# Gated recurrence: the last multiplication of keys and queries moved from VectorE to ScalarE, block by block

## The chip, the cores and the metric

The kernel runs on one core of a Trainium2 chip. Its engines work side by side, each through its own list of instructions, and they wait for each other through semaphores: PE (TensorE, matrix products), DVE (VectorE), ACT (ScalarE), POOL (GpSimd) and SP (SyncE, which here only starts transfers). The metric is the device time of one execution in microseconds (us); the time of a kernel is the median of its runs.

## What is computed

One step of a two-layer decoder, for 1024 prompt tokens and 8 x 8 sample tokens. Layer 0 runs stick-breaking attention and, beside it, a gated recurrence (HGRN2) of 4 heads with 128 key and 128 value channels; layer 1 is retention. The change touches the recurrence alone:

```python
def gla_chunk_scan(q, k, v, log_f, s0, chunk):
    def step(S, inp):
        qc, kc, vc, gc = inp
        bcum = jnp.cumsum(gc, axis=2)
        o_inter = jnp.einsum('bhtk,bhkv->bhtv', qc * jnp.exp(bcum), S)
        diff = bcum[:, :, :, None, :] - bcum[:, :, None, :, :]
        decay = jnp.exp(jnp.where(mask, diff, -jnp.inf))
        scores = jnp.einsum('bhtk,bhsk,bhtsk->bhts', qc, kc, decay)
        o_intra = jnp.einsum('bhts,bhsv->bhtv', scores, vc)
        blast = bcum[:, :, -1, :]
        S_new = jnp.exp(blast)[..., None] * S + jnp.einsum('bhsk,bhsv->bhkv', kc * jnp.exp(blast[:, :, None, :] - bcum), vc)
        return S_new, o_inter + o_intra
```

A key is multiplied by all gates that follow it in its chunk, a query by all gates up to it. The gates `f` stand per channel and token.

## The kernel before

The program is a row of stages, each closed by a barrier of all engines: input projection of layer 0, attention, the recurrence (`hgrn_now`, some 134 us from 839.7 to 973.9 us of the profiled execution), then the output projection of layer 0 together with the input projection of layer 1, and last retention with its output projection.

In `hgrn_now` the channels lie on the 128 partitions and the tokens along the rows: `k[h]`, `q[h]`, `f[h]` are 128 x 1088 (1024 prompt tokens, 64 sample tokens). A chunk has 128 tokens, so there are NCH = 8. The decay between two tokens is never formed. Instead the scores are computed in NLEV = 8 levels. Level 0 takes each token with itself. Between levels, `move(h, j)` on DVE (L1747 to L1753) multiplies, in every block of 2 x 2^j tokens, the keys of the first half by the product of the gates of the second half, and the queries of the second half by the product of the gates of the first half. The products of 2^j gates stand in `e[h]`, where POOL has built them (`first.products`). Level i then gives the scores between the two halves of blocks of 2^i tokens: on PE into `near` (levels 0 to 5) or `far` (6 and 7), and DVE (`pick`) or ACT copies them out. After level 7 comes `move(h, 6)`, the last, by the products of 64 gates: from then on a key carries all gates up to the end of its chunk, and a query all from the start. These are what the state of the recurrence needs. Head 0 has its tensors in the tile `first_place`; the others in `hg_k`, `hg_qd`, `hg_e`. The queries as moved are `qd`.

What follows a head's levels is its `rest(h)`: PE turns the keys (L1878, L1882, into `ku`), ACT copies them to `kd_tm` (L1711, L1716) and puts far and picked scores in place (L1713, L1720, L1723), PE makes the updates of the state (L1889) and of the samples' states (L1895), DVE chains them (`states`, L1787 and L1790, L1795), PE makes the outputs (L1905, L1907 and, for the samples, L1920 and L1922), and a norm over each head goes ACT (squares, L1693), PE (sums, L1865), ACT (L1702, L1704), DVE (`finish`, L1777, L1779).

The order is written out by hand, and is the same list on every engine: heads start 4 levels apart, so level i of head h stands beside level i + 4 of head h - 1. `run` goes through it and puts one piece of `rest` behind each level: `rest(0)` runs with heads 1 and 2, `rest(1)` begins when head 3 begins, `rest(2)` when head 3 is alone (two pieces to a level), and `rest(3)` follows at the end. Before a new `rest` begins, the one before is finished. An engine works strictly down its list, so what stands behind a waiting instruction waits too. In `rest(h)` PE waits for the last move of the keys before it turns them (L1870), and for that of the queries before the outputs (L1899).

Of the kernel before, what the change touches and what calls it, by code (L numbers as in the profile page):

```python
# [23 lines left out]
ACT = mybir.ActivationFunctionType  # L24
# [3 lines left out]
P = 128  # L28
# [797 lines left out]
class FirstHead:  # L826
# [7 lines left out]
    NM = 7  # L834
# [681 lines left out]
def hgrn_now(nc, first, q_fm, sig_fm, neg_fm, v_tm, gate_fm, out_gain, state_in, state_prompt, state_samples, mix_fm, consts):  # L1516
# [8 lines left out]
    with nc.cleanup_on_exit(), ExitStack() as ctx:  # L1525
# [3 lines left out]
        sem = lambda n: nc.alloc_semaphore(f"hg_{n}")  # L1529
        ps = lambda n, s: ctx.enter_context(nc.psum_tensor(f"hg_{n}", s, F32))  # L1530
        NM, NCH, NG = first.NM, TP // P, 2
# [25 lines left out]
        v_in, gate_in, s0_in = ([sem(f"{n}{h}") for h in range(HB)] for n in ("v_in", "g_in", "s_in"))  # L1557
        f_done, k_done, qd_done, e_done = first.f_done, first.k_done, first.qd_done, first.e_done
        scored, picked, k_moved, q_moved = sem("scored"), sem("picked"), sem("k_moved"), sem("q_moved")
        far_read, placed = sem("far_read"), sem("placed")  # L1560
        turned, held, updates, updates_s, state_done = sem("turned"), sem("held"), sem("updates"), sem("updates_s"), sem("state")
        vx_done, dec_done, s1_done, s_left = sem("vx"), sem("dec"), sem("s1"), sem("s_left")
# [7 lines left out]
        order = [(h, s - APART * h) for s in range(APART * (HB - 1) + NLEV) for h in range(HB) if 0 <= s - APART * h < NLEV]  # L1570
        nth = {x: i for i, x in enumerate(order)}
        nth_pick = {x: i for i, x in enumerate(x for x in order if x[1] < NPICK)}
        nth_move = {(h, i - 1): n for n, (h, i) in enumerate(x for x in order if x[1] >= 1)}

        def run(level, rest):

# [92 lines left out]
        @block.scalar  # L1669
        def _(act):  # L1670
            act.wait_ge(eps_set, 1)

            def level(h, i):
                if i == 0 and h + 1 < HB:
                    act.wait_ge(sig_in[h + 1], 16)
                    act.wait_ge(neg_in[h + 1], 16)
                    first.gates(nc, h + 1, f[h + 1][:], k[h + 1][:])
                if i == NLEV - 1:
                    s = scores[h % 2]
                    if h == 0:  # L1680
                        act.wait_ge(zeroed, 4)
                    if h >= 2:
                        act.wait_ge(o_done, 3 * (h - 1))
                    act.wait_ge(scored, nth[h, NLEV - 2] + 1)
                    for part, at in ((96, 0), (64, 64)):
                        nc.scalar.copy(s[at:at + 32, :, at + 32:at + 64], far[part:part + 32, :, 0:32]).then_inc(far_read, 1)

            def squares(h, g):
                src, _, tok = outputs_of(g)
                act.wait_ge(o_done, 3 * h + g + 1)  # L1690
                if h or g == 2:
                    act.wait_ge(sum_done, 3 * h + g - 1 if g else 3 * h)
                nc.scalar.activation(sq[g % 2][:, 0:tok.stop - tok.start], src, ACT.Square).then_inc(sq_done, 1)  # L1693

            def scales(h, g):

                _, total, tok = outputs_of(g)
                r = rs[g % 2][:, 0:tok.stop - tok.start]
                act.wait_ge(sum_done, 3 * h + g + 1)
                if h or g == 2:  # L1700
                    act.wait_ge(on_done, 3 * h + g - 1 if g else 3 * h)
                nc.scalar.activation(r, total, ACT.Ln, scale=1.0 / DB, bias=eps[:]).then_inc(ln_done, 1)  # L1702
                act.wait_ge(ln_done, 3 * h + g + 1)
                nc.scalar.activation(r, r, ACT.Exp, scale=-0.5).then_inc(rs_done, 1)  # L1704

            def rest(h):
                if h:
                    act.wait_ge(updates_s, NG * h)
                for g in range(NG):
                    act.wait_ge(turned, 3 * h + g + 1)  # L1710
                    nc.scalar.copy(kd_tm[:, 4 * g:4 * g + 4, :], ku[1 - g][:]).then_inc(held, 1)  # L1711
                act.wait_ge(scored, nth[h, NLEV - 1] + 1)
                nc.scalar.copy(scores[h % 2][0:64, :, 64:P], far[0:64, :, :]).then_inc(far_read, 1)  # L1713
                yield
                act.wait_ge(turned, 3 * h + 3)
                nc.scalar.copy(kd_tm[0:TS, NT - 1, :], ku[1][0:TS, 0, :]).then_inc(held, 1)  # L1716
                act.wait_ge(picked, nth_pick[h, NPICK - 1] + 1)
                for g in range(4):
                    at = slice(32 * g, 32 * g + 32)
                    nc.scalar.copy(scores[h % 2][at, :, at], picks[h][at, 0:NCH, :]).then_inc(placed, 1)  # L1720
                for g in range(2):
                    at = slice(32 * g, 32 * g + 32)
                    nc.scalar.copy(scores_s[h % 2][at, at], picks[h][at, NCH, :]).then_inc(placed, 1)  # L1723
                yield
                yield
                yield
                squares(h, 0)
                squares(h, 1)
                yield
                scales(h, 0)  # L1730
                yield
                scales(h, 1)
                squares(h, 2)
                yield
                scales(h, 2)

            run(level, rest)

        @block.vector
        def _(dve):  # L1740
# [22 lines left out]
                dve.copy_predicated(picks[h][:, 0:NCH, :], mask.unsqueeze(1).to_broadcast([P, NCH, 32]), near[n % 2][:, 0:NCH, :]).then_inc(picked, 1)  # L1763

            def level(h, i):
                if i >= 1:
                    move(h, i - 1)
                if i < NPICK:
                    pick(h, i)
# [57 lines left out]
        def _(pe):  # L1827
# [39 lines left out]
            def rest(h):  # L1867
                if h == 0:
                    pe.wait_ge(const_in, NCONST)
                pe.wait_ge(k_moved, nth_move[h, NM - 1] + 1)  # L1870
                if h:
                    pe.wait_ge(s1_done, NG * h)
                for g in range(NG):
                    if h and g:
                        pe.wait_ge(ln_done, 3 * h - 1)
                    for c in range(4):
                        at = 4 * g * P + c * P
                        mm = pe.transpose(ku[1 - g][:, c, :], k[h][:, at:at + P], ident[:])  # L1878
                    mm.then_inc(turned, 1)
                yield  # L1880
                pe.wait_ge(held, 3 * h + 1)
                pe.transpose(ku[1][0:TS, 0, :], k[h][:, TP:T], ident[:]).then_inc(turned, 1)  # L1882
                pe.wait_ge(v_in[h], 32)
                for g in range(NG):
                    if h:
                        pe.wait_ge(on_done, 3 * h - 2 + g)
                    pe.wait_ge(held, 3 * h + g + 1)
                    for c in range(4):
                        mm = pe.matmul(o[g][:, c, :], kd_tm[:, 4 * g + c, :], v[h][:, 4 * g + c, :], start=True, stop=True)  # L1889
                    mm.then_inc(updates, 1)  # L1890
                yield
                pe.wait_ge(held, 3 * h + 3)
                pe.wait_ge(vx_done, h + 1)
                for g in range(NG):
                    pe.matmul(ku[g][:].rearrange("p c n -> p (c n)"), kd_tm[0:TS, NT - 1, :],  # L1895
                              vx[:, 4 * g:4 * g + 4, :].rearrange("t c n -> t (c n)"), start=True, stop=True).then_inc(updates_s, 1)
                yield
                yield
                pe.wait_ge(q_moved, nth_move[h, NM - 1] + 1)  # L1899
                pe.wait_ge(placed, 6 * (h + 1))  # L1900
                pe.wait_ge(far_read, 3 * (h + 1))
                pe.wait_ge(state_done, NCH * (h + 1))
                for c in range(NCH):
                    tok = slice(c * P, c * P + P)
                    mm = pe.matmul(o[c // 4][:, c % 4, :], v[h][:, c, :], scores[h % 2][:, c, :], start=True, stop=True)  # L1905
                    if c:
                        mm = pe.matmul(o[c // 4][:, c % 4, :], state[:, c, :], qd[h][:, tok], start=False, stop=True, skip_group_check=True)  # L1907
                    if c % 4 == 3:
                        mm.then_inc(o_done, 1)
                yield  # L1910
                if h:
                    pe.wait_ge(mixed, 3 * h)
                sums(h, 0)
                pe.wait_ge(s1_done, NG * (h + 1))
                sums(h, 1)
                yield
                pe.wait_ge(ln_done, 3 * h + 1)
                pe.wait_ge(s0_in[h], 16)
                out = outputs_of(NG)[0]
                pe.matmul(out, v[h][0:TS, NT - 1, :], scores_s[h % 2][:], start=True, stop=True)  # L1920
                for c in range(NS):
                    mm = pe.matmul(out[:, c * LS:c * LS + LS], s0[h][:, c, :], qd[h][:, TP + c * LS:TP + c * LS + LS],  # L1922
                                   start=False, stop=True, skip_group_check=True)
                mm.then_inc(o_done, 1)
                yield
                sums(h, NG)
# [756 lines left out]
```

## Time and profile before

| | |
|---|---|
| median of 3 runs | 2126.63 us (2121.48 to 2128.65) |
| profiled execution, its own time | 2128.96 us |
| span of the profile | 2127.2 us |
| mean granted clock of TensorE | 0.938 |
| busy: PE / DVE / ACT / POOL | 1911.8 / 858.6 / 522.5 / 593.6 us |
| busy in the recurrence, 839.7 to 973.9 us | 94.3 / 85.3 / 43.2 / 37.8 us |
| granted clock there | 0.74 |

The durations come from one execution, the profiled one: its span is 1.8 us shorter than its own time, and that is 2.3 us above the median. A change of the stage is judged by what its last transfer does, since the barrier behind it holds everything that follows.

### The profile page before, as it was taken

The numbers are of one execution on the slowest core, as the hardware profiler recorded it, in microseconds if no ns is written. First come the engines' busy times: TensorE is split into PE (matmuls) and PEld (weight loads), VectorE is DVE, ScalarE is ACT, GpSimd is POOL, SyncE is SP. The second block draws the span as 40 slices with busy tenths as digits, with TensorE's granted clock in tenths as the row PEclk, the third lists the DMA queues.
The fourth block names the chain that finished last, engine by engine and source line by source line (L and its number), as shares of the span: only waits on it lengthen the run. The fifth ranks groups of instructions, "written<-read, shape, count | busy, mean of one in ns | idle before, by whom it ended". The sixth has DMA issues, their size and how long they took to land. (4 is left out here: it accounts for less than half of the span.)

```text
span 2127.2 us, 31286 instructions
## 1 busy us (share of the span) xinstructions
PE 1911.8 (90%) x11538; PEld 1532.9 (72%) x11538; DVE 858.6 (40%) x1480; ACT 522.5 (25%) x1133; POOL 593.6 (28%) x532
## 2 busy tenths in 40 slices
PE   6999999967787786686999999999999769999998
PEld 5788998954444553575889998887888547777776
DVE  3551000047787445663445442111000145656564
ACT  4210110145565432242430000000111132333231
POOL 3332222025565202513044222223330042212120
PEclk9999999978988998688999999999999879999999
DMA  4233232052233364515533333222231496655543
GB/s 146 83 109 104 82 114 90 36 173 72 74 112 99 99 197 153 168 54 173 165 110 102 92 88 102 90 87 84 92 100 48 122 261 199 210 176 188 189 153 124
DMA packets 210237, 261.56 MB, mean 123 GB/s; under 512 B 24260, under 2 KB 150916, under 8 KB 209860
## 3 DMA queue, kind: packets, MB, share of 16 engines
q1 hardware_dynamic: 153860, 198.94, 30.1%
q10 hardware_dynamic: 54256, 55.73, 8.0%
q0 software_dynamic: 2000, 5.25, 0.8%
q8 instruction: 80, 1.31, 0.3%
q14 instruction: 41, 0.34, 0.1%
HBM read 176.10 MB, written 81.40 MB: 121 GB/s over the span
## 5 line engine op out<-in xcount | busy, mean ns | idle before, releaser
L343 PE MATMUL odd_bank<-odd_w_hi,odd_h_hi 128*128 128x512 f32 x576 | 224.9, 390 | 2.5 <-DVE odd_shared L695 2.5
L343 PE MATMUL odd_bank<-odd_w_lo,odd_h_hi 128*128 128x512 f32 x576 | 224.6, 390 | 0.0
L343 PE MATMUL odd_bank<-odd_w_hi,odd_h_lo 128*128 128x512 f32 x512 | 199.8, 390 | 0.0
L291 POOL CAST odd_w_hi<-odd_raw 128x1024 fp32r<-128x1024 f32 x48 | 51.5, 1072 | 337.6 <-PE odd_bank L343 313.6
L343 PE MATMUL even_bank<-even_h_hi,even_w_hi 128*128 128x362 f32 (+1 forms) x384 | 127.2, 331 | 4.4 <-DVE even_stage_tm L695 4.4
L343 PE MATMUL odd_bank<-odd_h_hi,odd_w_hi 128*128 128x362 f32 (+1 forms) x384 | 126.0, 328 | 1.8 <-POOL odd_w_lo L293 1.8
L343 PE MATMUL even_bank<-even_h_lo,even_w_hi 128*128 128x362 f32 (+1 forms) x384 | 127.3, 331 | 0.0
L343 PEld LDWEIGHTS odd_bank<-odd_w_hi,odd_h_hi 128*128 128x128 f32 x576 | 108.5, 188 | 25.4 <-DVE odd_shared L695 2.9
L343 PE MATMUL even_bank<-even_h_hi,even_w_lo 128*128 128x362 f32 (+1 forms) x384 | 126.8, 330 | 0.0
L343 PE MATMUL odd_bank<-odd_h_lo,odd_w_hi 128*128 128x362 f32 (+1 forms) x384 | 126.0, 328 | 0.0
L343 PE MATMUL odd_bank<-odd_h_hi,odd_w_lo 128*128 128x362 f32 (+1 forms) x384 | 125.0, 326 | 0.0
L343 PEld LDWEIGHTS odd_bank<-odd_w_lo,odd_h_hi 128*128 128x128 f32 x576 | 108.6, 188 | 22.4
L343 PE MATMUL even_bank<-even_w_hi,even_h_hi 128*128 128x512 f32 x288 | 114.7, 398 | 7.1 <-DVE even_head_n L686 4.4
L293 POOL TENSOR_TENSOR odd_w_lo<-odd_raw,odd_w_hi 128x1024 fp32r<-128x1024 f32 x48 | 115.8, 2412 | 3.8
L343 PE MATMUL even_bank<-even_w_lo,even_h_hi 128*128 128x512 f32 x288 | 113.8, 395 | 0.0
L343 PEld LDWEIGHTS odd_bank<-odd_w_hi,odd_h_lo 128*128 128x128 f32 x512 | 96.5, 188 | 20.2
L990 POOL CAST ap_k_hi<-first_place 128x512 fp32r<-128x512 f32 (+3 forms) x96 | 48.4, 504 | 200.9 <-DVEq L1131 136.8
L2281 PE MATMUL rt_y<-rt_w_hi,rt_m_hi 128*128 128x512 f32 x256 | 103.3, 404 | 0.0
L343 PE MATMUL even_bank<-even_w_hi,even_h_lo 128*128 128x512 f32 x256 | 101.2, 395 | 0.0
L291 POOL CAST even_w_hi<-even_raw 128x1024 fp32r<-128x1024 f32 x32 | 33.8, 1057 | 239.2 <-PE even_bank L343 199.0
L2281 PE MATMUL rt_y<-rt_w_hi,rt_m_lo 128*128 128x512 f32 x256 | 100.0, 391 | 0.0
L2281 PE MATMUL rt_y<-rt_w_lo,rt_m_hi 128*128 128x512 f32 x256 | 99.8, 390 | 0.0
(328 smaller groups left out, 4108.5 us busy)
## 6 DMA issues: line engine op xcount, KB each, us to landing
odd_raw<-in_w_in_odd SPq DMA_DIRECT2D x48, 512.0 KB, 3.8
even_raw<-in_w_in_even SPq DMA_DIRECT2D x32, 512.0 KB, 3.8
k_page<-in_cache_k SPq DMA_DIRECT2D x64, 256.0 KB, 3.1
v_page<-in_cache_v SPq DMA_DIRECT2D x64, 256.0 KB, 3.1
rt_s<-in_state_ret SPq DMA_DIRECT2D x32, 512.0 KB, 6.0
out_ret_sample<-rt_s SPq DMA_DIRECT2D x32, 512.0 KB, 3.2
v_tm<-odd_shared ACTq DMA_DIRECT2D x64, 128.0 KB, 2.0
g_tm<-odd_shared ACTq DMA_DIRECT2D x64, 128.0 KB, 1.9
```

The costliest lines, as they stand in the source:

```text
L291: nc.gpsimd.tensor_copy(hi, r).then_inc(w_hi_done, 1)
L293: nc.gpsimd.tensor_tensor(lo, r, hi.bitcast(F32), ALU.subtract).then_inc(w_split, 1)
L343: mm = pe.matmul(out, stationary, moving, start=(j == 0), stop=(j == len(pairs) - 1))
L990: nc.gpsimd.tensor_copy(k_hi[:, m, lo:NQ], sums[:, i % NX, lo:NQ]).then_inc(carry_hi, 1)
L2281: mm = pe.matmul(yp[half][:], a[:, r, :], b[:, r, cols], start=(r == 0 and j == 0), stop=(r == R - 1 and j == len(ops) - 1))
```

## The change

`move(h, 6)` leaves DVE's list. In its place a new function `last_move(h)` stands first in ACT's `rest(h)`. It does the same products in 16 instructions, one for each chunk and each of the two operands, of 128 partitions x 64 tokens: a Copy with a scale, where the scale is the column of `e[h]` that holds the product of 64 gates, one number for each partition. The eight of the keys come first and end with a semaphore of their own, `k_last`; the eight of the queries follow and end with `q_last`. PE waits for these two where it waited for DVE.

```diff
-        nth_move = {(h, i - 1): n for n, (h, i) in enumerate(x for x in order if x[1] >= 1)}
+        nth_move = {(h, i - 1): n for n, (h, i) in enumerate(x for x in order if 1 <= x[1] < NLEV - 1)}
...
+            def last_move(h):
+
+                ends = first.blocks(f[h], e[h], NM - 1)
+                act.wait_ge(scored, nth[h, NLEV - 1] + 1)
+                act.wait_ge(k_moved, nth_move[h, NM - 2] + 1)
+                act.wait_ge(q_moved, nth_move[h, NM - 2] + 1)
+                act.wait_ge(e_done, NM * (h + 1))
+                for t, half, moved in ((k[h], 0, k_last), (qd[h], 1, q_last)):
+                    for c in range(NCH):
+                        at, factor = slice(c * P + 64 * half, c * P + 64 * half + 64), 2 * c + 1 - half
+                        ins = nc.scalar.activation(t[:, at], t[:, at], ACT.Copy, scale=ends[:, factor:factor + 1])
+                    ins.then_inc(moved, 1)
+
             def rest(h):
+                last_move(h)
                 if h:
                     act.wait_ge(updates_s, NG * h)
...
             def level(h, i):
-                if i >= 1:
+                if 1 <= i < NLEV - 1:
                     move(h, i - 1)
...
-                pe.wait_ge(k_moved, nth_move[h, NM - 1] + 1)
+                pe.wait_ge(k_last, h + 1)
...
-                pe.wait_ge(q_moved, nth_move[h, NM - 1] + 1)
+                pe.wait_ge(q_last, h + 1)
```

On DVE, where head 0 ends its levels and head 1 stands at its level 4 (`first_place` with 128x8x64 is the last move of head 0), before:

```order
L1763 COPY_PREDICATED hg_picks1<-first_mask,hg_near0 128x256
L1752 TENSOR_TENSOR first_place<-first_place 128x8x64
L1753 TENSOR_TENSOR first_place<-first_place 128x8x64
L1752 TENSOR_TENSOR hg_k1<-hg_k1,hg_e1 128x136x4
L1753 TENSOR_TENSOR hg_qd1<-hg_qd1,hg_e1 128x136x4
L1762 COPY_PREDICATED hg_picks1<-first_mask,hg_near1 64x32
```

and after:

```order
L1778 COPY_PREDICATED hg_picks1<-first_mask,hg_near0 128x256
L1767 TENSOR_TENSOR hg_k1<-hg_k1,hg_e1 128x136x4
L1768 TENSOR_TENSOR hg_qd1<-hg_qd1,hg_e1 128x136x4
L1777 COPY_PREDICATED hg_picks1<-first_mask,hg_near1 64x32
L1778 COPY_PREDICATED hg_picks1<-first_mask,hg_near1 128x256
```

The two multiplications of head 0 are gone, and the next move of head 1 stands directly behind the pick.

On ACT, where the norm of head 1's samples ends and `rest(2)` begins, before:

```order
L1693 ACTIVATE hg_sq0<-hg_ss 128x64
L1702 ACTIVATE hg_rs0<-hg_ss,hg_eps 128x64
L1704 ACTIVATE hg_rs0<-hg_rs0 128x64
L1711 COPY hg_kd_tm<-hg_ku1 128x512
L1711 COPY hg_kd_tm<-hg_ku0 128x512
```

and after:

```order
L1694 ACTIVATE hg_sq0<-hg_ss 128x64
L1703 ACTIVATE hg_rs0<-hg_ss,hg_eps 128x64
L1705 ACTIVATE hg_rs0<-hg_rs0 128x64
L1717 ACTIVATE hg_k2<-hg_k2,hg_e2 128x64 x8
L1717 ACTIVATE hg_qd2<-hg_qd2,hg_e2 128x64 x8
L1726 COPY hg_kd_tm<-hg_ku1 128x512
L1726 COPY hg_kd_tm<-hg_ku0 128x512
```

Sixteen instructions stand between the norm of head 1 and the copies of head 2's turned keys; it is the same in front of the copies of the other heads.

## Rows read from the trace of the kernel before

**Rows 1.** Timeline, end of the stage: start, duration, engine, line, operation.

```profile
970.12 0.33 SPq L1635 DMA_DIRECT2D mix<-hg_mix  x1
973.87 0.34 SPq L260 DMA_DIRECT2D odd_stage_rot<-in_w_out_even  x1
```

**Rows 2.** Timeline of ACT: rows of short instructions, with their total duration.

```profile
72.31 1.82 ACT L487 ACTIVATE even_h_hi<-even_turn,even_gain 128x64 fp32r<-128x64 f32 x8 [5.20 <-PE even_turn L337]
...
956.12 1.68 ACT L1720 COPY hg_scores<-hg_picks 32x256 f32<-32x256 f32 x4
```

**Rows 3.** Groups by line and form, ACT: count, busy us, mean ns, idle before.

```profile
L1083 ACT ACTIVATE first_place<-first_place 128x512 f32<-128x512 f32 x48 | 30.3, 631 | 1.5
...
L1083 ACT ACTIVATE first_place<-first_place 128x128 f32<-128x128 f32 x16 | 5.0, 310 | 0.5
...
L860 ACT ACTIVATE hg_k<-hg_k,first_half 128x1088 f32<-128x1088 f32 x3 | 3.6, 1188 | 0.0
...
L487 ACT ACTIVATE even_h_hi<-even_turn,even_gain 128x64 fp32r<-128x64 f32 x8 | 1.8, 315 | 5.2 <-PE even_turn L337 5.2
```

**Rows 4.** Timeline of DVE, around the last moves of heads 0 and 1.

```profile
869.81 2.04 DVE L1752 TENSOR_TENSOR first_place<-first_place 128x512 f32<-128x512 f32 x1 [0.41 <-PE hg_far L1858]
871.78 1.57 DVE L1753 TENSOR_TENSOR first_place<-first_place 128x512 f32<-128x512 f32 x1
...
878.71 2.38 DVE L1753 TENSOR_TENSOR hg_qd<-hg_qd,hg_e 128x512 f32<-128x512 f32 x1
...
898.87 0.69 DVE L1752 TENSOR_TENSOR hg_k<-hg_k,hg_e 128x512 f32<-128x512 f32 x1 [3.59 <-PE hg_far L1858]
...
901.68 0.72 DVE L1752 TENSOR_TENSOR hg_k<-hg_k,hg_e 128x544 f32<-128x544 f32 x1 [1.52 <-PE hg_near L1845]
```

**Rows 5.** Timeline of POOL beside the DVE instructions of head 0.

```profile
868.66 2.65 POOL L873 TENSOR_TENSOR hg_qd<-hg_q,hg_f 128x1088 f32<-128x1088 f32 x1 [5.20 <-ACT hg_f L859]
...
878.14 2.39 POOL L1665 TENSOR_TENSOR hg_s_dec<-hg_s,first_place 128x1024 f32<-128x1024 f32 x1
```

**Rows 6.** Timeline of PE: levels, turned keys and updates of heads 0 to 3.

```profile
875.38 1.08 PE L1845 MATMUL hg_near<-hg_qd,hg_k 128*32 128x32 f32 x64 [3.88 <-DVE hg_k L1752]
...
879.26 1.97 PE L1878 MATMUL hg_ku<-hg_ident,first_place 128*128 128x128 f32 x8
...
908.41 0.30 PE L1882 MATMUL hg_ku<-hg_ident,hg_k 128*64 128x128 f32 x1
...
933.96 1.98 PE L1889 MATMUL hg_o<-hg_v,hg_kd_tm 128*128 128x128 f32 x16
...
942.39 0.63 PE L1907 MATMUL hg_o<-hg_qd,hg_state 128*128 128x128 f32 x2
...
955.10 3.10 PE L1889 MATMUL hg_o<-hg_v,hg_kd_tm 128*128 128x128 f32 x16
...
960.87 0.39 PE L1907 MATMUL hg_o<-hg_qd,hg_state 128*128 128x128 f32 x2
```

**Rows 7.** Timeline of ACT: norm's last instruction and first copies, heads 1 to 3.

```profile
905.16 0.26 ACT L1704 ACTIVATE hg_rs<-hg_rs 128x64 f32<-128x64 f32 x1
906.17 1.07 ACT L1711 COPY hg_kd_tm<-hg_ku 128x512 f32<-128x512 f32 x2 [0.76 <-PE hg_ku L1878]
...
931.42 0.26 ACT L1704 ACTIVATE hg_rs<-hg_rs 128x64 f32<-128x64 f32 x1
933.19 1.27 ACT L1711 COPY hg_kd_tm<-hg_ku 128x512 f32<-128x512 f32 x2 [1.51 <-PE hg_ku L1878]
...
954.09 0.26 ACT L1704 ACTIVATE hg_rs<-hg_rs 128x64 f32<-128x64 f32 x1
954.26 0.57 ACT L1711 COPY hg_kd_tm<-hg_ku 128x512 f32<-128x512 f32 x1
```

**Rows 8.** Busy time and granted clock by stretch (PEclk: third figure from the end).

```profile
core 0: us, PE busy (x) PEld busy (x) DVE busy (x) ACT busy (x) POOL busy (x), PEclk, DMA share, GB/s
...
932.00:934.00 2.00, 2.00 (x14) 1.72 (x10) 1.86 (x5) 0.72 (x2) 0.00 (x0) 0.60 0.25 92
...
955.00:957.00 2.00, 2.00 (x10) 2.00 (x11) 0.70 (x3) 1.95 (x6) 0.00 (x0) 0.50 0.50 199
```

More of the change, by code:

```diff
@@ L1559, in hgrn_now @@
         scored, picked, k_moved, q_moved = sem("scored"), sem("picked"), sem("k_moved"), sem("q_moved")
+        k_last, q_last = sem("k_last"), sem("q_last")
         far_read, placed = sem("far_read"), sem("placed")
```

## Prediction

> **What bounds the kernel now.** The change lies in one stage, so I asked first what a delay there would cost. The timeline at its end shows the last transfer of the stage at 970.12 us and the next stage's first one at 973.87, 3.8 us later [rows 1]. The barrier lets nothing pass, so a microsecond more or less at the last transfer is one at the end of the kernel. Then I read the stage engine by engine. No engine is full in it; it is a relay of waits. The reader should look at three things. On DVE, what ended the wait before each move: for head 1's last move it was PE's far scores, and after it DVE waits again for PE, 1.52 us [rows 4]. On ACT, how soon after the norm of one head the copies of the next head's turned keys begin: 0.8 us for head 1, 1.5 for head 2, none for head 3 [rows 7]. On PE, what stands behind these copies: the samples' turned keys and the updates [rows 6]. The updates feed DVE's chain of states, and that the outputs; so a late copy is a late head.
>
> **What a piece costs on ACT.** The trace has no 128x64 Copy from SBUF to SBUF with a scale from memory, so I bound it. Nearest is the cast of the input projection, 8 instructions of 128x64 with such a scale, reading PSUM: 315 ns each, 8 in 1.82 us [rows 2, 3], so start to start (1.82 - 0.315) / 7 = 0.215 us; they overlap by 0.10. For SBUF, L860 is the same operation at 1088 columns, 1188 ns; the slope from L1083 is (631 - 310) / 384 = 0.836 ns a column, which leaves 1188 - 1024 x 0.836 = 332 ns at 64 columns [rows 3]. With the overlap of 0.10 that is 0.235 us a piece. Sixteen: 3.76 us until the next instruction can start, of which the keys are 8 x 0.235 + 0.10 = 1.98 us. Lower bound 0.215 (3.44 us), upper bound 0.332, no overlap at all, as the four small copies of L1720 show none (1.68 us for four [rows 2]): 5.3 us. I take 0.235, since the same operation and the same width overlap. The Trainium skill, "ScalarE: Activation LUTs", What ACT_TABLE_LOAD costs, gives 186 ns plus 0.833 a column, 93 more for a scale from memory and 93 of overlap: an estimate of 0.24 us a piece, 3.8 us in all, by which the sum would be the same within 0.3 us. The same page's rules for kernel authors say that a multiplication belongs on VectorE; here the row agrees, since DVE does each operand in 0.69 us [rows 4] where ACT needs 1.98, and what decides is only who waits for which.
>
> **What leaves DVE.** Eight instructions, two a head. For heads 1 to 3 they bring nothing: DVE had been waiting for PE before them and waits for it, or for ACT, behind them [rows 4]; the 0.69 us each lies in idle time. For head 0 they cost more than they look: 2.04 and 1.57 us, against 0.69 for the same form later [rows 4]. Beside them POOL works on head 3's products; the first move ends at 871.85, POOL's instruction from 868.66 at 871.31. The second case is clearer: DVE's 2.38 us from 878.71 end at 881.09, POOL's from 878.14 at 880.53 [rows 4, 5]. Each time DVE ends 0.55 us after POOL, about its own undisturbed length. So the two take turns, and the pair removed held DVE for 3.5 us while head 1's next move stood behind it; PE waited 3.88 us for that [rows 6]. How much comes back? DVE can't start the next move before PE's scores of that level, it meets POOL's next instructions instead, and PE then has its own work: its turning of head 0 ends at 881.23, and the next level begins at 881.59 [rows 6]. If PE's list moves not at all, only 0.36 us comes back. At most it is 3.5 us and one later turn with POOL less (2.38 - 0.69 = 1.7), 5.2 us. The other way, an unlucky turn with POOL, I allow 0.5. I take 1.0 us gained, near the small end, because PE is nearly gapless there. ACT's pieces for head 0 cost nothing: ACT idles there until PE has turned the keys at 879.26 [rows 6], and in the 10 us before that they fit twice over.
>
> **What arrives on ACT for heads 1 to 3.** `last_move(h)` stands behind the norm of head h - 1, however early the far scores were. The first piece can start 0.09 us before the norm's last instruction ends.
> - Head 1: pieces from 905.33. PE gets its keys at 907.3 and turns them; the first copy starts at 905.33 + 3.76 = 909.09 (before: 906.17) and ends 0.57 later, as head 3's does [rows 7], at 909.66. PE's samples' keys, which wait for it, started at 908.41 and now start at 909.75: **+1.3 us** [rows 6, 7].
> - Head 2: from 931.59, first copy at 935.35 (before: 933.19). The updates started at 933.96, right behind that copy, so all is passed on: **+2.2 us** [rows 6, 7].
> - Head 3: from 954.26, where the first copy stood; it moves by the whole of the sixteen: **+3.8 us** [rows 7]. PE has turned the keys before 958 in either case, so the queries' eight, which nobody needs yet, cost as much as the keys' eight.
>
> The added waits themselves are free: scores, moves and products of head h are done by then. Behind the pieces on ACT stand the copies, the far and the picked scores; the latter are needed only when DVE's states are done, later than they come. The sum so far is 1.3 + 2.2 + 3.8 - 1.0 = +6.3 us.
>
> **The clock of PE.** New gaps arise, about 2 us before the turning and 1 us before the updates. What such gaps do is seen in the stage: head 3's eight updates take 3.10 us where head 2's take 1.98 [rows 6], and the granted clock in 955 to 957 us is 0.50, the 1.2 GHz level, while PE is busy all the time [rows 8]. It was at 0.60 in 932 to 934 too [rows 8], just before head 2's updates, which now start after a gap. Bounds: nothing; or head 1's and head 2's updates at the low level (some 1.1 us each, 3.10 - 1.98, up to 1.5) and head 3's outputs too, 15 products at 0.43 apart instead of 0.22 (from rows 0.63 and 0.39 long [rows 6]), 3 us: 6 us in all. I take head 2's updates alone, **+1.5 us**. Sum: **+7.8 us**. Against the profiled execution's own 2128.96 us this makes 2136.8; the median lies 2.3 us below it, so I forecast 2126.63 + 7.8 = **2134.4 us**.
>
> **The rivals.**
> - *DVE and POOL come apart* (not slower). Its place is head 0 and 1, 870 to 882 us; its price is up to 5.2 us gained. It decides from the point where PE isn't held by its own work at 881. For it: the 3.88 us wait of PE, the largest of a move. Against: PE's 0.36 us of slack. Time: 2126.63 + 7.3 - 5.2 = 2128.7, no difference. The Trainium skill, "SBUF — State Buffer", SBUF: two separate sides, calls the port of the two an exclusive lock held for a whole instruction, and names ACT's own port free of it; by that rule, with which the rows' 0.55 us agree, taking work from DVE here frees POOL as well.
> - *ACT's pieces don't overlap*: 16 x 0.097 = 1.55 us more a head, three times 4.7: 2139.1.
> - *The clock stays low*: 6 in place of 1.5: 2138.9. For it: the stage's mean granted clock is 0.74 already, the span's 0.938; against: head 1's turning comes after busy work.
> - *The clock falls well*: a shift lets the outputs of a head that ran at 0.43 apart run at 0.22, 3 us a head for two heads, and the gain of head 0 reaches 5.2. 2126.63 + 6.3 + 1.0 - 5.2 - 6 = 2122.7. Little speaks for it.
>
> **How the numbers follow.** Within 0.3%, some 6.4 us, a measurement of this kernel can't tell a change from none. Forecast 0.60, DVE and POOL 0.15, no overlap 0.10, clock low 0.10, clock well or other 0.05. The forecast's own spread (0.215 a piece: -1.0; head 0: +1.5 to -2; clock -1.5 to +2) puts a third of it under +6.4. So slower 0.41 + 0.20 = 0.61; same 0.19 + 0.15 = 0.34; faster 0.05. The range reaches from the second case (2128.7, less a little for the scatter of the runs) to just over the slow ones: 2128.0 to 2141.5.
>
> **What the next profile would show.** Right: ACT with sixteen 128x64 instructions in 3.6 to 4.0 us behind each norm, heads 1 to 3 with first copies 2.9, 2.2 and 3.8 us further behind it; DVE without the pair; stage 6 to 9 us longer, most of it after head 2. Wrong: pieces at 0.3 us or more; head 1's level 4 on PE more than 2 us earlier, the sign of the DVE and POOL rival; updates of heads 2 and 3 at 1.98 us, which would say that the gaps don't lower the clock. What would overturn it all is work in a later stage that sheds the shift, which the barrier makes unlikely.

## The result and the profile after

The changed kernel takes 2133.76 us in the median of 15 runs (2128.62 to 2143.15), the kernel before, in the same series, 2126.28 us (2120.51 to 2131.95). The medians differ by 7.5 us. The ratio of the runs is 1.0038, 95% interval 1.0028 to 1.0049, or 8.1 us (6.0 to 10.4). The change is small, but clear of the noise: the kernel is slower, and 2134.4 us was forecast. Here and below, the us behind a ratio are worked out from it, and are not the difference of the two medians.

The profiled execution took 2132.56 us. From its page, engine by engine:

```profile
span 2130.8 us, 31346 instructions
...
PE 1911.3 (90%) x11538; PEld 1532.1 (72%) x11538; DVE 852.3 (40%) x1472; ACT 537.6 (25%) x1197; POOL 594.0 (28%) x532
```

DVE has eight instructions and 6.3 us less, ACT 64 instructions and 15.1 us more: 0.24 us for each of them. The span grew by only 3.6 us, less than the median. What happened in the stage must therefore be read in the stage. On ACT, the norm of one head, then the last move, then the copies of the next head's turned keys, for heads 1 to 3; it answers to [rows 7]:

```profile
904.50 0.26 ACT L1705 ACTIVATE hg_rs<-hg_rs 128x64 f32<-128x64 f32 x1
904.66 2.00 ACT L1717 ACTIVATE hg_k<-hg_k,hg_e 128x64 f32<-128x64 f32 x8
906.57 2.01 ACT L1717 ACTIVATE hg_qd<-hg_qd,hg_e 128x64 f32<-128x64 f32 x8
908.48 1.04 ACT L1726 COPY hg_kd_tm<-hg_ku 128x512 f32<-128x512 f32 x2
...
931.73 0.26 ACT L1705 ACTIVATE hg_rs<-hg_rs 128x64 f32<-128x64 f32 x1
...
935.72 1.04 ACT L1726 COPY hg_kd_tm<-hg_ku 128x512 f32<-128x512 f32 x2
...
955.71 0.26 ACT L1705 ACTIVATE hg_rs<-hg_rs 128x64 f32<-128x64 f32 x1
...
959.69 1.04 ACT L1726 COPY hg_kd_tm<-hg_ku 128x512 f32<-128x512 f32 x2
```

From the start of the norm's last instruction to the first copy it is now 3.98, 3.99 and 3.98 us; before it was 1.01, 1.77 and 0.17 [rows 7]. The sixteen pieces take 908.48 - 904.66 = 3.82 us, 0.239 each from start to start. The copies are 2.97, 2.2 and 3.8 us further behind; the forecast said 2.9, 2.2 and 3.8.

PE in the same places (answers to [rows 6]):

```profile
877.99 0.76 PE L1860 MATMUL hg_near<-hg_q,hg_k 128*32 128x32 f32 x38 [3.06 <-issue]
878.68 1.97 PE L1893 MATMUL hg_ku<-hg_ident,first_place 128*128 128x128 f32 x8
...
906.72 1.97 PE L1893 MATMUL hg_ku<-hg_ident,hg_k 128*128 128x128 f32 x8 [1.50 <-ACT hg_k L1717]
908.62 1.08 PE L1860 MATMUL hg_near<-hg_qd,hg_k 128*32 128x32 f32 x64
909.63 0.38 PE L1897 MATMUL hg_ku<-hg_ident,hg_k 128*64 128x128 f32 x1
...
936.33 0.42 PE L1897 MATMUL hg_ku<-hg_ident,hg_k 128*64 128x128 f32 x1 [0.41 <-ACT hg_kd_tm L1726]
936.55 3.64 PE L1904 MATMUL hg_o<-hg_v,hg_kd_tm 128*128 128x128 f32 x16
...
957.93 1.97 PE L1893 MATMUL hg_ku<-hg_ident,hg_k 128*128 128x128 f32 x8 [2.60 <-ACT hg_k L1717]
960.31 0.42 PE L1897 MATMUL hg_ku<-hg_ident,hg_k 128*64 128x128 f32 x1 [0.41 <-ACT hg_kd_tm L1726]
960.52 3.64 PE L1904 MATMUL hg_o<-hg_v,hg_kd_tm 128*128 128x128 f32 x16
```

What ended PE's idle time in front of the turning (L1893) is now the last move on ACT, and, at heads 2 and 3, in front of L1897 the copy on ACT. The updates (L1904) of heads 2 and 3 take 3.64 us where they took 1.98 and 3.10 [rows 6]. A head has eight updates; the row counts each twice (x16). Below are two stretches of the changed kernel: head 2's updates, and the turning of head 3. The columns are the stretch, its length, busy time and instructions by engine (PE, PEld, DVE, ACT, POOL), then the granted clock as the third figure from the end, the DMA share and GB/s:

```profile
936.50:940.10 3.60, 3.60 (x17) 3.39 (x16) 0.00 (x0) 2.83 (x9) 0.00 (x0) 0.50 0.00 0
...
957.90:960.00 2.10, 1.97 (x8) 1.57 (x8) 0.00 (x0) 2.10 (x9) 0.00 (x0) 0.50 0.00 0
```

**A ruler for the stage.** I cut the stage at PE's outputs (L1905 before, L1920 after). The first figure is head 0 from its last far scores to its outputs. The next three are the legs to the outputs of heads 1, 2 and 3, each from the end of the outputs before. Then the lengths of the outputs of heads 0, 1 and 2; from the start of head 3's outputs the stage needs 9.8 us more to its last transfer (10.0 in e5). The whole stage is counted from head 0's last far scores to that transfer. In the profile of before, for example, head 2's outputs begin at 941.40 and head 3's at 960.35; head 2's last 6.37, so the leg of head 3 is 12.58. All fourteen profiles, in us (the experiments are told below):

| profile | head 0 | leg 1 | leg 2 | leg 3 | outputs 0, 1, 2 | whole stage |
|---|---|---|---|---|---|---|
| before | 24.71 | 20.12 | 17.33 | 12.58 | 5.22, 6.19, 6.37 | 102.3 |
| before, 2nd (e9) | 24.71 | 20.14 | 16.30 | 12.75 | 5.22, 4.95, 3.58 | 97.4 |
| before, 3rd (e10) | 24.67 | 19.54 | 17.33 | 12.58 | 5.03, 6.34, 6.44 | 101.7 |
| changed | 24.83 | 22.47 | 21.41 | 16.77 | 5.22, 5.22, 3.59 | 109.3 |
| changed, 2nd (e11) | 23.19 | 24.02 | 20.03 | 17.01 | 5.22, 6.40, 5.19 | 110.9 |
| changed, 3rd (e12) | 24.19 | 21.50 | 21.10 | 16.73 | 5.16, 5.22, 3.59 | 107.3 |
| e1, heads 1 to 3 | 24.69 | 21.50 | 21.09 | 16.71 | 5.11, 5.22, 3.59 | 107.7 |
| e2, head 3 | 24.43 | 19.57 | 17.26 | 16.72 | 5.22, 6.50, 4.93 | 104.4 |
| e3, queries late | 23.02 | 22.44 | 19.53 | 16.25 | 5.22, 5.22, 5.16 | 106.6 |
| e4, head 0 | 23.40 | 20.26 | 16.30 | 12.84 | 5.22, 5.15, 3.59 | 96.5 |
| e5, more pieces | 23.16 | 26.19 | 23.25 | 18.34 | 5.22, 5.22, 3.59 | 114.9 |
| e6, PE kept busy | 22.96 | 21.49 | 20.19 | 15.48 | 5.22, 5.22, 5.00 | 105.3 |
| e7, POOL waits | 23.68 | 19.57 | 16.29 | 12.75 | 5.21, 4.97, 3.59 | 95.8 |
| e8, head 0 and POOL waits | 22.99 | 20.09 | 16.30 | 12.73 | 5.22, 4.93, 3.59 | 95.6 |

Over three profiles each, the stage grew from 100.5 to 109.2 us, 8.7 us: legs 1, 2 and 3 by 2.7, 3.9 and 4.2, less 0.6 at head 0 and 1.5 in the outputs. That is the whole slowdown, and a little more. It is a mean of few profiles with a wide scatter: the unchanged kernel alone has 97.4 and 102.3. What lies ahead of the ruler scatters as well: head 0's last far scores start between 864.5 and 868.6 us in the three profiles of the kernel before, and between 860.2 and 871.5 in all fourteen.

### The profile page after: what moved, and what is told of

Its sections match the earlier page's. It is cut to its first block and busy times, and to the rows that moved or that the text cites. A ratio compares the mean times of both kernels' runs of the same rounds, so it can differ in the third digit from the quotient of the medians.

```text
span 2130.8 us, 31346 instructions
## 1 busy us (share of the span) xinstructions
PE 1911.3 (90%) x11538; PEld 1532.1 (72%) x11538; DVE 852.3 (40%) x1472; ACT 537.6 (25%) x1197; POOL 594.0 (28%) x532
## 5 line engine op out<-in xcount | busy, mean ns | idle before, releaser
L343 PEld LDWEIGHTS odd_bank<-odd_w_hi,odd_h_lo 128*128 128x128 f32 x512 | 96.5, 189 | 20.2
L992 POOL TENSOR_TENSOR ap_k_lo<-first_place,ap_k_hi 128x512 fp32r<-128x512 f32 (+3 forms) x96 | 97.5, 1016 | 7.7
```

The source lines that it names most:

```text
L343: mm = pe.matmul(out, stationary, moving, start=(j == 0), stop=(j == len(pairs) - 1))
L992: nc.gpsimd.tensor_tensor(k_lo[:, m, lo:NQ], sums[:, i % NX, lo:NQ], k_hi[:, m, lo:NQ].bitcast(F32), ALU.subtract).then_inc(carry_split, 1)
```

## The experiments

The theories: Q, the queue on ACT in front of the copies makes heads 1 to 3 late; C, the time is that of PE's clock, lowered by the new gaps; D, the relief of DVE and POOL at head 0 gives much back; A and B, whether the differences between profiles of one kernel are chance or belong to it. All ratios are against the kernel before in the same series; e5 to e8 ran on another chip than e1 to e4 and e9 to e12.

### e1, e2 and e4: which head costs what

A tuple says whose last move is on ACT: (1, 2, 3) in e1, (3,) in e2, (0,) in e4.

```diff
-                if 1 <= i < NLEV - 1:
+                if i >= 1 and not (h in ON_ACT and i == NLEV - 1):
                     move(h, i - 1)
...
-                last_move(h)
+                if h in ON_ACT:
+                    last_move(h)
...
-                pe.wait_ge(k_last, h + 1)
+                pe.wait_ge(*((k_last, ON_ACT.index(h) + 1) if h in ON_ACT else (k_moved, nth_move[h, NM - 1] + 1)))
```

> Heads 1 to 3 as in the changed kernel, head 0's last move back on VectorE. Theory Q (the sixteen ScalarE pieces of 0.236 us stand in front of the copies of the turned keys, and each head is late by what of them the copies and then TensorE feel: 1.3, 2.2 and 3.8 us, plus a microsecond or two of low clock): +7 to +9 us against the kernel before, as the whole change or a little more. Theory D (head 0's relief of VectorE and GpSimd gives back 3 us or more): this one loses it, +10 to +12. Theory C (the time is that of TensorE's clock, which the new gaps lower, and not of the queue): the same +7.5, but with the copies of head 3 less than 2 us later behind the norm.

Measured: 2134.69 us against 2126.04, ratio 1.0057 (1.0038 to 1.0076), 12.1 us (8 to 16). The legs are those of the changed kernel (21.50, 21.09, 16.71), and head 0 is that of before (24.69). So the cost lies in heads 1 to 3. The time alone would rather speak for D's +10 to +12 than for Q's +7 to +9, though its interval reaches down to 8. The stage speaks for Q: at 107.7 us it is 7.2 longer than the mean of the kernel before, and the head 0 column bounds what is lost there at 1 to 2 us.

> Only head 3's last move on ScalarE; heads 0 to 2 on VectorE as before. Theory Q: +3.8 us from the queue alone, up to +5 with the updates at the low clock (3.64 us in place of 3.10). Theory C: the cost needs the gaps of heads 1 and 2, so under +2. Head 3's first copy starts 3.8 us further behind the norm's last instruction than before under Q.

Measured: 2125.88 us against 2126.04, ratio 1.0009 (0.9993 to 1.0024), 1.9 us (-1.5 to +5.1). The time can't tell Q's 3.8 from C's less than 2. The profile can:

```profile
948.51 0.26 ACT L1706 ACTIVATE hg_rs<-hg_rs 128x64 f32<-128x64 f32 x1
948.67 2.00 ACT L1718 ACTIVATE hg_k<-hg_k,hg_e 128x64 f32<-128x64 f32 x8
950.58 2.01 ACT L1718 ACTIVATE hg_qd<-hg_qd,hg_e 128x64 f32<-128x64 f32 x8
952.49 1.05 ACT L1728 COPY hg_kd_tm<-hg_ku 128x512 f32<-128x512 f32 x2
```

The copy stands 3.98 us behind the norm's last instruction, as Q says, and leg 3 alone is long: 16.72 against 12.6 to 12.8, with legs 1 and 2 as before. The whole stage, 104.4 us, is 4.0 above the mean of the kernel before. The cost of head 3 needs no gap of an earlier head.

> Only head 0's last move on ScalarE; heads 1 to 3 on VectorE as before. Theory Q: nothing is in front of a copy that matters, and TensorE's list is nearly gapless at the turning of head 0: 0 to -1 us. Theory D: -3 us or more, with head 1's level 4 on TensorE 2 us earlier and the gain kept until the states of head 0.

Measured: 2120.56 us against 2126.04, ratio 0.9983 (0.9966 to 0.9999), -3.6 us (-7.2 to -0.2). By time alone D's -3 fits better than Q's 0 to -1. The profile speaks against D: head 0 takes 23.40 us in place of 24.4 to 24.7, about the one microsecond of Q and of the forecast, and head 1's level 4 starts 6.29 us after head 0's last far scores, where it was 7.55 before: 1.3 us earlier, not 2. The rest of the measured gain isn't in that column. It is taken up at the end of this section.

### e3: the queries' pieces behind the copies

```diff
             def rest(h):
-                last_move(h)
+                last_move(h, 0)
...
                     nc.scalar.copy(scores_s[h % 2][at, at], picks[h][at, NCH, :]).then_inc(placed, 1)
+                last_move(h, 1)
                 yield
```

> The changed kernel, but the eight pieces of the queries stand on ScalarE behind the copies of the turned keys and the picked scores, ahead of the outputs that need them. Theory Q, read finely: what remains is TensorE's wait for the eight pieces of the keys, 1.9 to 2.0 us before it may turn them: head 1 +0.9, head 2 +1.7, head 3 +2.8, in all +5.4 against before, 2 us better than the changed kernel. If every piece in the queue counts alike, half of 7.5 goes: +3.7. Theory C: no difference from the changed kernel, since the gap before the turning stays.

Measured: 2131.22 us against 2126.04, ratio 1.0035 (1.0017 to 1.0053): 7.4 us (3.6 to 11.3). By its median it lies between the changed kernel and before, but the intervals don't tell it from the changed kernel, nor Q's +5.4 from the other forecasts. The profile, ACT and then PE at head 3:

```profile
953.02 0.26 ACT L1705 ACTIVATE hg_rs<-hg_rs 128x64 f32<-128x64 f32 x1
953.18 2.00 ACT L1717 ACTIVATE hg_k<-hg_k,hg_e 128x64 f32<-128x64 f32 x8
956.44 0.59 ACT L1726 COPY hg_kd_tm<-hg_ku 128x512 f32<-128x512 f32 x1 [1.26 <-PE hg_ku L1894]
```

```profile
955.24 1.97 PE L1894 MATMUL hg_ku<-hg_ident,hg_k 128*128 128x128 f32 x8 [2.60 <-ACT hg_k L1717]
...
957.30 2.38 PE L1905 MATMUL hg_o<-hg_v,hg_kd_tm 128*128 128x128 f32 x16
...
962.61 0.71 PE L1921 MATMUL hg_o<-hg_scores,hg_v 128*128 128x128 f32 x4 [1.03 <-ACT hg_qd L1717]
```

With the queries gone from the front, the copy comes only 3.42 us after the norm's last instruction, in place of 3.98: now ACT waits for PE's turning, which waits for the keys' eight. Against the mean of the changed kernel's profiles the legs are 0.2, 1.3 and 0.6 us shorter, 2.1 in all, where the finer form of Q said 0.4, 0.5 and 1.0. The sum agrees, the heads don't, so the sum is partly luck. Two things that Q left out are in these rows. The updates of heads 2 and 3 took 2.4 us here, where they took 3.64 in the changed kernel's first profile. And at head 3 the queries' pieces, now late, are what the outputs wait for (1.03 us, L1921). What is shown is that the two halves of the queue aren't two equal costs: with the queries' eight away from the front, the copy came only 0.56 us earlier, since it then waited for PE's turning, which took 1.97 us at the low clock.

### e5: eight pieces more

```diff
+                for c in range(NCH):
+                    nc.scalar.activation(spare[:, 64 * c:64 * c + 64], ones[:, 0:64], ACT.Copy, scale=ends[:, c:c + 1])
```

> The changed kernel with eight more ScalarE pieces of 128x64 in each head's last move, in front of the copies (products of ones into a spare tile that nobody reads). Theory Q: 8 x 0.236 = 1.9 us more in front of the copies of heads 1 to 3, all of it felt (also by head 1, whose slack is used up): +5.7 us against the changed kernel, +13 against before. Theory C: the gaps are there already and the clock is low in them, so less than +3 more.

Measured: 2140.09 us against 2125.72, ratio 1.0074 (1.0058 to 1.0091), 15.7 us (12.3 to 19.3), where Q said +13. That is 7.6 us above the changed kernel by the ratios, and the stage is 5.8 us longer than its mean. Q's 5.7 fits, C's less than 3 doesn't. From the norm to the copies it is 5.90 us:

```profile
896.53 0.26 ACT L1706 ACTIVATE hg_rs<-hg_rs 128x64 f32<-128x64 f32 x1
...
900.52 2.00 ACT L1723 ACTIVATE hg_spare<-hg_ones,hg_e 128x64 f32<-128x64 f32 x8
902.43 1.04 ACT L1731 COPY hg_kd_tm<-hg_ku 128x512 f32<-128x512 f32 x2
```

It is 1.9 us more at each of the three heads. The legs don't take it up evenly: they are 3.5, 2.4 and 1.5 us longer than the mean of the changed kernel. Leg 1 grows most, since its updates take 3.64 us here. Whether the longer gap brought the low clock there isn't shown: in the changed kernel's own three profiles they took 1.95, 3.37 and 1.99.

### e6: PE kept busy in the gap

```diff
                 if h:
                     pe.wait_ge(s1_done, NG * h)
+                    for _ in range(6):
+                        pe.matmul(ku[1][:, 0, :], ident[:], ident[:], start=True, stop=True)
+                pe.wait_ge(k_last, h + 1)
```

> The changed kernel, with six more products of the identity with itself (128x128) on TensorE in heads 1 to 3, into a bank that is free, in the gap before it may turn the keys. Theory C: the clock stays at its full level, the updates of heads 2 and 3 take 1.98 us again in place of 3.64, and the kernel gains about 3 us. Theory Q: the copies stand where they stood; the updates may be faster, but the outputs of head 2, which ran at full clock just after the slow updates, pay it back: within 1.5 us of the changed kernel.

Measured: 2129.5 us against 2125.72, ratio 1.0021 (1.0010 to 1.0032), 3.6 us less than the changed kernel's 1.0038 (1.0028 to 1.0049); the intervals overlap a little. The stage agrees: 105.3 us, 3.8 below the changed kernel's mean. PE at head 2 and at head 3:

```profile
934.92 2.10 PE L1906 MATMUL hg_o<-hg_v,hg_kd_tm 128*128 128x128 f32 x16
936.95 0.76 PE L1860 MATMUL hg_near<-hg_qd,hg_k 128*32 128x32 f32 x64
...
956.02 1.09 PE L1895 MATMUL hg_ku<-hg_ident,hg_k 128*128 128x128 f32 x8 [1.21 <-ACT hg_k L1717]
958.40 0.30 PE L1899 MATMUL hg_ku<-hg_ident,hg_k 128*64 128x128 f32 x1 [1.29 <-ACT hg_kd_tm L1726]
```

The updates take 2.10 and 1.98 us, the turning of head 3 1.09 in place of 1.97, and the granted clock is 1.00 from 957 to 964 us. The copies stand where they stood, 3.98 us behind the norm, at heads 1 and 3. At head 2 the filling did less: the clock was low there already, the six products took 2.93 us (1.56 at head 3) and held the turning back, that took 1.92 us, and the copy came 4.43 us behind the norm. So both theories hold a part. As an estimate from the two ratios, of some 8 us about 3.5 are the clock's, and about 4.5 are left with PE mostly at the full clock. C's forecast of 3 came nearer here than Q's 1.5.

### e7 and e8: GpSimd out of VectorE's way

In e7 the last moves are all on DVE; in e8 head 0's is on ACT. In both POOL waits:

```diff
                 if h == 0:
                     pool.wait_ge(const_in, NCONST)
+                    pool.wait_ge(q_moved, nth_move[1, 3] + 1)
```

> The kernel before in everything (all last moves on VectorE), but GpSimd waits with head 0's two products of rest (its spreading of the samples' values and its decay of their states, 1.9 and 2.4 us) until VectorE has done head 1's move by products of 8 gates. If VectorE and GpSimd take turns, that pair takes 0.7 us each in place of 2.26 and 2.38, 3.3 us less on VectorE. Theory D: the kernel gains 2 to 3 us. Theory Q: TensorE's own list bounds the place, its next level can't start before its turning of head 0 has ended: 0 to -1 us.

Measured: 2121.55 us against 2125.72, ratio 0.9984 (0.9970 to 0.9999), -3.4 us (-6.4 to -0.2). On DVE, in e7:

```profile
879.00 0.69 DVE L1770 TENSOR_TENSOR hg_k<-hg_k,hg_e 128x512 f32<-128x512 f32 x1 [0.78 <-PE hg_near L1863]
879.61 0.68 DVE L1771 TENSOR_TENSOR hg_qd<-hg_qd,hg_e 128x512 f32<-128x512 f32 x1
```

The first of the two in the profile of before (the second is in [rows 4]):

```profile
876.52 2.26 DVE L1752 TENSOR_TENSOR hg_k<-hg_k,hg_e 128x512 f32<-128x512 f32 x1 [0.79 <-PE hg_near L1845]
```

On PE, in e7:

```profile
881.05 0.76 PE L1863 MATMUL hg_near<-hg_q,hg_k 128*32 128x32 f32 x38 [1.69 <-issue]
881.74 1.97 PE L1896 MATMUL hg_ku<-hg_ident,first_place 128*128 128x128 f32 x8
883.64 0.93 PE L1863 MATMUL hg_near<-hg_qd,hg_k 128*32 128x32 f32 x64
```

The pair takes 0.69 and 0.68 us where the same one took 2.26 and 2.38 before: that DVE waited for POOL is shown, by taking POOL's work away. The Trainium skill ("SBUF — State Buffer", SBUF: two separate sides) calls it an exclusive lock held for a whole instruction. The rows agree: before, the pair's second instruction ended 0.56 us after POOL's [rows 4, 5]. But head 0 gains only 1.0 us of the 3.3: PE's next level follows its own turning at once, 883.64 behind 881.74 + 1.97. In this place Q's bound holds, not D's. By time alone, D's 2 to 3 us fits the 3.4 better.

> Head 0's last move alone on ScalarE, and the same wait of GpSimd. Both reliefs of VectorE together: Theory D: -4 us or more against before. Theory Q: TensorE bounds the place: 0 to -1.5 us.

Measured: 2119.8 us against 2125.72, ratio 0.9977 (0.9965 to 0.9990), -4.9 us (-7.4 to -2.1). That is D's forecast by time, and outside Q's. Head 0 takes 22.99 us, 1.7 less than before, and that is near Q's; the other 3 us aren't in that column. Of all versions this has the lowest ratio, though its interval overlaps those of e4 and e7: head 0's last move on ACT, where no copy is late by it, the others on DVE, and POOL held back.

### e9 to e12: the same kernels again

> The kernel before, unchanged, profiled once more, because its first profile had the outputs of heads 1 and 2 at the low clock (6.2 and 6.4 us long) where the kernels with head 0 on ScalarE had 5.0 and 3.6. Theory A (the clock's phase is chance from run to run, and the profile of before was an unlucky one): other lengths here, the stage 98 to 101 us from head 0's last far scores to the last transfer, in place of 102.3. Theory B (it belongs to the kernel): again about 6.2 and 6.4, stage 102.

Measured: 2119.77 us in its one execution. Head 2's outputs, in this profile and with the granted clock of the stretch below it:

```profile
935.81 0.68 PE L1905 MATMUL hg_o<-hg_scores,hg_v 128*128 128x128 f32 x4 [2.22 <-DVE hg_state L1790]
936.33 0.39 PE L1907 MATMUL hg_o<-hg_qd,hg_state 128*128 128x128 f32 x2
```

```profile
935.80:939.40 3.60, 3.59 (x31) 3.60 (x32) 2.25 (x4) 0.60 (x1) 1.18 (x1) 1.00 0.16 48
```

In the first profile of before the same products began with this:

```profile
941.40 1.19 PE L1905 MATMUL hg_o<-hg_scores,hg_v 128*128 128x128 f32 x4 [2.22 <-DVE hg_state L1790]
```

and the stretch there had a granted clock of 0.50:

```profile
941.40:945.40 4.00, 4.00 (x19) 4.00 (x20) 2.26 (x4) 0.60 (x1) 1.57 (x1) 0.50 0.23 72
```

One program, the same wait of 2.22 us ahead: the outputs took 3.58 us or 6.37 us. Theory A. The stage, 97.4 us, is even shorter than A's 98 to 101.

> The same again, a third profile of the kernel before: Theory A: a length that differs from at least one of the other two; Theory B: 6.2 and 6.4 us, stage 102.

Measured: 2129.41 us; outputs of 6.34 and 6.44 us, the slow kind again, and a stage of 101.7 us. With the second profile that makes two kinds of execution among three, 97.4 and 102 us of stage. The kernel's own spread of 2117 to 2132 us has at least this cause, but not it alone: the second profile's time is 9.2 us below the first's, of which the stage holds 4.9 and what lies ahead of the ruler 3.3.

> The changed kernel, unchanged, profiled once more. Its first profile gave nothing back at head 0 (24.8 us from the last far scores to the outputs, as before), where five other kernels with head 0 relieved took 23.0 to 23.7. If the relief is the rule, about 23 us here. Stage 107 to 110 us, updates of heads 2 and 3 3.64 us again (Theory B for them), or shorter in one of the looks (Theory A).

Measured: 2135.79 us. Head 0 at 23.19 us: the relief is there. The stage, 110.9 us, is a little over the 107 to 110 expected. Updates of 3.37, 2.44 and 3.64 us at heads 1, 2 and 3: which of the heads meets the low clock isn't fixed.

> The same again, a third profile of the changed kernel: head 0 at about 23 us; sixteen pieces between the norm and the copies in 3.8 us as in every profile.

Measured: 2135.71 us. Head 0 at 24.19, nearer to before than to 23; the pieces as always (first copies 3.98 to 3.99 us behind the start of the norm's last instruction). Over the seven profiles with head 0's move on ACT and POOL unchanged the mean is 23.54, against 24.64 over the five with it on DVE: 1.1 us. Over the changed kernel's own three it is 24.07, 0.6 less than before. Head 1 in this profile:

```profile
908.68 1.09 PE L1893 MATMUL hg_ku<-hg_ident,hg_k 128*128 128x128 f32 x8 [1.88 <-ACT hg_k L1717]
...
911.07 0.30 PE L1897 MATMUL hg_ku<-hg_ident,hg_k 128*64 128x128 f32 x1 [0.60 <-ACT hg_kd_tm L1726]
```

Here the turning took 1.09 us after a wait of 1.88, where it took 1.97 after one of 1.50 in the first profile. A gap of that length isn't always followed by the low clock. And here it is the copy that L1897 waits for.

What stays open is the rest of the gains of e4, e7 and e8. Head 0 accounts for 1.0 to 1.7 us of 3.4 to 4.9; all three profiles show the outputs of heads 1 and 2 of the quick kind. Executions below 2122 us were 8 of 12 in e4 (8 of 30 for before in that series), 7 of 12 and 10 of 12 in e7 and e8 (5 of 29). So the shift may have changed how often the clock is low in the outputs. With one profile of each that isn't shown, nor why it should be so.

## Why the prediction was right

- **The stage ends the argument: right.** The next stage's first transfer stands at 979.72 us, 3.8 behind the last of this one, as before [rows 1]. What follows takes 1151.1 to 1153.9 us in all the profiles, without order by kernel. In the first pair it was 2.3 us less for the changed kernel, and what lies ahead of the ruler 1.2 less, which is why the span grew by 3.6 us only, where the stage grew by 7.0.
- **The price of a piece: right.** 0.235 us forecast, 0.239 measured; the rival without overlap (0.332) is out. The estimate of 0.24 that was worked out from the Trainium skill ("ScalarE: Activation LUTs", What ACT_TABLE_LOAD costs) is met as well.
- **Heads 2 and 3: right.** The queue's 2.2 and 3.8 us are in the profile to a tenth. Part of that exactness is the choice of the profile: in the second one of before the copies stood 0.99 and 0.56 us behind the norm, and against it the shifts are 3.0 and 3.4. Leg 3 grew by 4.2, and the rest over the queue's 3.8 is put down to the clock, which is argued; leg 2 grew by 3.9, against 2.2 + 1.5 forecast. One reading was wrong: that the queries' eight cost head 3 as much as the keys' eight. With them away from the front (e3) the copy gained 0.56 us, not 1.9.
- **Head 1: mis-sized.** The forecast let 1.3 us through, because PE's own level stood in between. It was 2.7 in the mean of three. The term that was left at nothing is the clock at head 1: in two of the three profiles the turning took 1.97 us at the low clock (1.09 before, from 905.43) and the next level 1.08, and it was they, not the copy, that held L1897 (909.63 in the first). In the third, with the turning at 1.09, the copy held it, as forecast, and the leg is 1.6 us over the mean of before.
- **Head 0: about right.** 1.0 us gained was forecast, 1.1 is the mean over seven profiles, 0.6 over the changed kernel's own three. In its first profile nothing came back: head 1's level 4 did start 0.8 us earlier, but a wait of PE that no row explains ("issue") grew from 1.69 to 3.06 us and ate the lead. The rival that DVE and POOL come apart had the mechanism right (e7) and the price wrong: PE's list is the bound. Its sign, head 1's level 4 more than 2 us earlier, didn't appear; it was 0.8 to 1.3 in the changed kernel's profiles. Its time of 2128.7 also left out the clock's 1.5 us; with them it would have been 2130.2.
- **The clock: right sum, wrong account.** +1.5 us was put on head 2's updates, and there it is: 3.64, 2.44 and 3.64 us in three profiles against 1.98. But it also came at head 1, and partly at head 3 (3.64 against 3.10, 2.33 and 3.13), and it left the outputs, where the kernel before had lost 4.2 to 4.3 us in two of three profiles: 1.5 us less there. The term that was left out was what the clock already cost before. e6 puts the clock's share at some 3.5 of 8 us; the forecast had 1.5 of 7.8.
- **The sum.** 2134.4 forecast, 2133.8 measured. In the stage, over three profiles each, it was 8.7 against 7.8. Two errors of about 1.5 us, in head 1's leg and in the outputs, cancelled; that the sum came out to half a microsecond is luck.

## What to carry to other kernels

An instruction sequence moved to an idle engine is paid where it stands in that engine's list, not by how idle the engine is: these sixteen pieces held ACT for 3.8 us at every head, which made the copies 2.2 to 3.8 us late at three of them and nothing late at head 0. Ask for each place separately what the list has next and who waits for it; the same edit was worth having at one head of four. And where a stage is a relay of waits, profile the same kernel more than once before costing anything to a tenth: here one unchanged program had a stage of 97.4 and of 102.3 us, with 4.0 of the difference in outputs at one clock or the other.

## What the runs showed of the hardware

- Eight updates, products of 128x128 in 32-bit floats, took 1.95 to 1.99 us at a granted clock of 1.00 (2.4 GHz) and 3.64 us at 0.50, which is 1.2 GHz; turning eight blocks of 128x128 took 1.09 and 1.97 us.
- After a wait of 2.60 us for ACT the turning ran at the low level in all seven profiles that have one. After waits of 1.49 to 1.91 us it did so in ten cases and ran at the high level in two (e1 and e12, 1.88 us). Head 0's turning ran low in all fourteen profiles, with no wait directly before it. With six products put into the gap it ran high at heads 1 and 3 and low at head 2.
- After identical waits of 2.22 us, head 2's outputs of the unchanged kernel ran at the low clock in two executions and at the high one in a third.
- ACT's 128x64 instructions in place, with a scale from memory, go at 0.239 us from start to start; they overlap a little, since eight are recorded with 2.00 us where 8 x 0.239 is 1.91.
- DVE's products of two tensors in SBUF waited out a product on POOL, and the wait is inside their recorded length: 2.26 and 2.38 us beside it, 0.69 and 0.68 without.
